# Delta-rule heads: the second weight tile's split ahead of the exponents' arguments, and the three engines' orders around it

## What is computed

```python
q, k, v = silu(conv(h @ w_q)), silu(conv(h @ w_k)), silu(conv(h @ w_v));  z = silu(h @ w_z)
q, k = l2norm(q) * 128**-0.5, l2norm(k)
gam = exp(G[t] - G[s]) below the diagonal          # G: running sum of the log decay in a chunk
A = strict(beta * (k @ k.T) * gam);  attn = (q @ k.T) * gam
X = inverse(I + A)                                 # u0 = X @ (v*beta), w = X @ (k*beta*exp(G))
for each chunk t:                                  # the state S is carried from chunk to chunk
    u = u0 - w @ S;  o = (q*exp(G)) @ S + attn @ u;  S = exp(G_last)*S + (k*exp(G_last-G)).T @ u
out = rmsnorm(o) * g_head * z
```

## Time and profile before

| | value |
|---|---|
| median of three runs | 1972.1 us |
| the profiled execution | 1974.02 us |
| its span, from first to last instruction | 1972.3 us |
| TensorE busy in the span | 1716.7 us (87%) |
| VectorE busy | 909.3 us (46%) |
| ScalarE busy | 614.8 us (31%) |
| GpSimd busy | 225.4 us (11%) |
| mean granted TensorE clock | 0.935 |

### The profile page before, as it was taken

One profiled execution on the slowest core, in us unless ns is written; L12 is line 12 of the kernel. 1 busy time (PEld: TensorE's weight loads), 2 busy tenths in 40 slices (PEclk: granted clock), 3 DMA queues, 4 the chain that ended last, 5 costly groups with the idle time before them and its releaser, 6 DMA issues. The chain is left out here.

```text
span 1972.3 us, 32281 instructions
## 1 busy us (share of the span) xinstructions
PE 1716.7 (87%) x11328; PEld 1496.0 (76%) x11328; DVE 909.3 (46%) x2004; ACT 614.8 (31%) x1523; POOL 225.4 (11%) x481
## 2 busy tenths in 40 slices
PE   6875999999699999899389997899899899877797
PEld 1124888888699999699278887888788788766696
DVE  0043344443355454512555554566566557563422
ACT  0033232322222322423533442333333333331422
POOL 0010000000000000000100000033133223222000
PEclk9986999999799999899688998999999999998798
DMA  6642241222223321141232211311111111010322
GB/s 243 233 142 64 60 113 49 74 54 69 62 61 82 96 53 53 33 133 43 73 90 73 70 32 49 89 34 49 36 36 45 36 36 45 4 37 1 95 86 69
DMA packets 194512, 138.16 MB, mean 70 GB/s; under 512 B 13310, under 2 KB 188346, under 8 KB 192262
## 3 DMA queue, kind: packets, MB, share of 16 engines
q1 hardware_dynamic: 179464, 127.76, 22.6%
q10 hardware_dynamic: 14976, 9.45, 1.6%
HBM read 126.06 MB, written 11.13 MB: 70 GB/s over the span
## 5 line engine op out<-in xcount | busy, mean ns | idle before, releaser
L160 PE MATMUL bank<-hT_low,gdn_w_high 128*128 128x288 f32 x512 | 173.4, 339 | 40.8 <-DVE gdn_w_low L1335 37.7
L161 PE MATMUL bank<-hT_high,gdn_w_low 128*128 128x288 f32 x512 | 156.7, 306 | 0.0
L162 PE MATMUL bank<-hT_high,gdn_w_high 128*128 128x288 f32 x512 | 156.5, 306 | 0.0
L160 PE MATMUL bank<-output_gT_low,output_w_high 128*128 128x288 f32 x512 | 154.2, 301 | 0.0
L161 PE MATMUL bank<-output_gT_high,output_w_low 128*128 128x288 f32 x512 | 152.5, 298 | 0.0
L162 PE MATMUL bank<-output_gT_high,output_w_high 128*128 128x288 f32 x512 | 152.4, 298 | 0.0
L160 PEld LDWEIGHTS bank<-hT_low,gdn_w_high 128*128 128x128 f32 x512 | 101.7, 199 | 51.4 <-issue 27.9
L1713 POOL TENSOR_TENSOR gdn_A_level<-gdn_AT,const 128x128 f32<-128x128 f32 (+1 forms) x232 | 110.0, 504 | 188.5 <-DVE gdn_AT L1635 112.8
L161 PEld LDWEIGHTS bank<-hT_high,gdn_w_low 128*128 128x128 f32 x512 | 102.1, 199 | 0.0
L162 PEld LDWEIGHTS bank<-hT_high,gdn_w_high 128*128 128x128 f32 x512 | 101.6, 198 | 0.0
L233 PE MATMUL bank<-setup_w_ada,setup_silu_c 128*2 128x512 f32 x192 | 90.1, 624 | 13.1 <-DMA setup_w_ada<-in_w_ada 13.1
(11 more groups left out here) (444 smaller groups left out, 4651.9 us busy)
## 6 DMA issues: line engine op xcount, KB each, us to landing
x<-in_w_in_even SPq DMA_DIRECT2D x72, 512.0 KB, 4.1
x<-in_w_in_odd SPq DMA_DIRECT2D x56, 512.0 KB, 4.0
setup_w_ada<-in_w_ada SPq DMA_DIRECT2D x16, 1536.0 KB, 6.7
output_w_out<-in_w_out_even SPq DMA_DIRECT2D x28, 256.0 KB, 3.5
output_w_out<-in_w_out_odd SPq DMA_DIRECT2D x28, 256.0 KB, 3.4
gdn_E<-G_rows SPq DMA_DIRECT2D x8, 576.0 KB, 4.9
x<-in_x_prompt SPq DMA_DIRECT2D x2, 2048.0 KB, 9.4
out_y_p<-x SPq DMA_DIRECT2D x1, 2048.0 KB, 6.8
```

What stands on the lines that cost most here:

```text
L160: pe.matmul(out, w[0], x[1], start=first, stop=False)
L161: pe.matmul(out, w[1], x[0], start=False, stop=False)
L162: return pe.matmul(out, w[0], x[0], start=False, stop=last)
```

## The change

TensorE's items are dealt out anew: one more ahead of the k and q transposes, two fewer between the k products and the first inverse's transposes, one more in the levels, and the last two behind the recurrence's last products. On VectorE `low` of tile 1 goes right behind z, the arguments of the exponents go behind `kq_norm`, and the scaled copies of k and v go behind `attn_ready`. On ScalarE the exponents go behind the copies of k^T and q^T. Nothing is added or left out.

```diff
-    LEVEL_FILL = (39, 40, 42, 43, 44, 45, 46, 47, 48, 49, 50, 51, 52)
+    LEVEL_FILL = (38, 39, 40, 41, 43, 44, 45, 46, 48, 49, 50, 51, 52)
...
-            project(pe, ahead, 5, 22)
+            project(pe, ahead, 5, 23)
...
-            project(pe, ahead, 22, 26)
+            project(pe, ahead, 23, 27)
...
-            project(pe, ahead, 26, 37)
+            project(pe, ahead, 27, 36)
             pe.wait_ge(*s["XT1_ready"].done(h, 0))
             pe.wait_ge(*s["attn_ready"].done(h, 0))
...
-            project(pe, ahead, 37, 39)
+            project(pe, ahead, 36, 38)
...
-                project(pe, ahead, *((52, 55), (55, 58), (58, 60), (60, 62), (62, 64))[t])
+                project(pe, ahead, *((52, 55), (55, 58), (58, 60), (60, 61), (61, 62))[t])
...
                 pe.matmul(PS[7][0:R, P:2 * P], tiles(atT, t), u[0:R, :], start=True, stop=True).then_inc(s["o_psum"].sem, 1)
+                if t == PT:
+                    project(pe, ahead, 62, 64)
                 if t:
                     turn_g(pe, h, t - 1)
```

```diff
             take_projection(act, ahead, 0)
-            act.wait_ge(*s["arg_ready"].done(h, 0))
-            act.activation(E[:, :, 0:SEQ], E[:, :, 0:SEQ], ACT.Exp).then_inc(s["E_ready"].sem, 1)
-            act.activation(E[0:DEC, :, SEQ:TOK], E[0:DEC, :, SEQ:TOK], ACT.Exp).then_inc(s["E_ready"].sem, 1)
             take_projection(act, ahead, 1)
...
             last.then_inc(s["kq_copied"].sem, 1)
+            act.wait_ge(*s["arg_ready"].done(h, 0))
+            act.activation(E[:, :, 0:SEQ], E[:, :, 0:SEQ], ACT.Exp).then_inc(s["E_ready"].sem, 1)
+            act.activation(E[0:DEC, :, SEQ:TOK], E[0:DEC, :, SEQ:TOK], ACT.Exp).then_inc(s["E_ready"].sem, 1)
             take_projection(act, ahead, 2)
```

```diff
             dve.scalar_tensor_tensor(zs[:], tz, 1.0, zr, ALU.add, ALU.mult).then_inc(s["z_ready"].sem, 1)
 
+            low(dve, ahead, 1)
+
+            dve.wait_ge(*s["rn_ready"].done(h, 0))
...
+            dve.tensor_tensor(qn[:], tk[:, :, 0, :], spread(sc[:, 1, :]), ALU.mult).then_inc(s["kq_norm"].sem, 1)
+
             dve.wait_ge(*s["G_loaded"].done(h, 15))
...
             last.then_inc(s["arg_ready"].sem, 1)
 
-            dve.wait_ge(*s["rn_ready"].done(h, 0))
...
-            dve.tensor_tensor(qn[:], tk[:, :, 0, :], spread(sc[:, 1, :]), ALU.mult).then_inc(s["kq_norm"].sem, 1)
-            low(dve, ahead, 1)
-            dve.tensor_tensor(sc[:, 2, :], sc[:, 0, :], gcol(1), ALU.mult)
...
-            dve.tensor_tensor(bv[:], tk[:, :, 2, :], spread(gcol(2)), ALU.mult).then_inc(s["kv_scaled"].sem, 1)
             low(dve, ahead, 2)
...
             dve.tensor_tensor(atT[:, 0:SEQ], PS[3][:, :], E[:, 0, 0:SEQ], ALU.mult).then_inc(s["attn_ready"].sem, 1)
+
+            dve.tensor_tensor(sc[:, 2, :], sc[:, 0, :], gcol(1), ALU.mult)
+            dve.tensor_tensor(sc[:, 3, :], sc[:, 0, :], gcol(3), ALU.mult).then_inc(s["scale_b"].sem, 1)
+            dve.wait_ge(*s["scale_b"].done(h, 0))
+            dve.tensor_tensor(kbe[:], tk[:, :, 1, :], spread(sc[:, 2, :]), ALU.mult)
+            dve.tensor_tensor(kg[:], tk[:, :, 1, :], spread(sc[:, 3, :]), ALU.mult)
+            dve.tensor_tensor(bv[:], tk[:, :, 2, :], spread(gcol(2)), ALU.mult).then_inc(s["kv_scaled"].sem, 1)
+
             dve.wait_ge(*s["X1_copied"].done(h, 0))
```

More of the change, by code:

```diff
@@ L1622, in dve_turn @@
             dve.tensor_tensor(qn[:], tk[:, :, 0, :], spread(sc[:, 1, :]), ALU.mult).then_inc(s["kq_norm"].sem, 1)
-            low(dve, ahead, 1)
-            dve.tensor_tensor(sc[:, 2, :], sc[:, 0, :], gcol(1), ALU.mult)
[L1625 to L1628, removed]
-            dve.tensor_tensor(bv[:], tk[:, :, 2, :], spread(gcol(2)), ALU.mult).then_inc(s["kv_scaled"].sem, 1)
+            dve.wait_ge(*s["G_loaded"].done(h, 15))
+            for i, name in ((1, "neg_strict"), (0, "neg_causal")):
+                for t in range(T):
+                    R = rows(t)
+                    at = E[0:R, i, t * P:t * P + R]
+                    last = dve.scalar_tensor_tensor(at, at, M["Gcol"][0:R, t, bass.ds(h, 1)],
+                                                    M.c(name, R)[:, 0:R], ALU.subtract, ALU.add)
+            last.then_inc(s["arg_ready"].sem, 1)
             low(dve, ahead, 2)
```

## The result

The changed kernel takes 1945.6 us (median of four, 1944.13 to 1948.81) against 1971.65 us of the kernel before (four runs): a ratio of 0.9868, 95% interval 0.9851 to 0.9885. A second measurement on another occasion gave 0.9864 (0.9843 to 0.9886). It is faster, as forecast, but by 26 us and not by 35: 1945.6 lies above the range of 1931 to 1943.

A forecast was written before the change was run, and what follows sets the result against it. Seven heads were held limited by TensorE's own queue, stopped mostly by waits for tile 1. 29.7 + 10.9 - 2.8 - 2.8 + 0.3 = 35.3 us gained gave a forecast of 1936.5 us, range 1931 to 1943.

The forecast's parts named there:

- the normalised q ended more than 0.3 us after item 22: Sign of being wrong: q comes over 0.3 us behind the last TensorE item placed ahead of the k and q transposes.
- TensorE waits in the levels for the inverse's updates: Sign of being wrong: TensorE waits for VectorE's updates in the levels, where nothing was expected to be late.
- The split of tile 1: VectorE's split moves 4.24 us earlier, so TensorE's wait for the tile goes: 29.7 us gained over seven heads.
- The clock: TensorE's clock no longer falls behind the wait for tile 1: 1.55 us a head, 10.9 us over seven heads.
- k and q normalised: Ahead of the k transposes: `kq_norm` comes 0.25 us earlier, GpSimd's power covering the split; at worst 0.2 us a head lost.
- The scaled copies of k and v: Their 2.49 us on VectorE fit its idle time between attn and the levels; nothing late, no cost.
- VectorE late in the levels: Rival: GpSimd's masked copies stretch the moved copies by 1.18, at worst 0.7 us a head, 1941.4 us; chance 0.15.
- Nine items ahead of the first inverse: Nine items instead of eleven leave TensorE a new 0.4 us wait for attn in seven heads: 2.8 us cost.
- Recurrence: At the fourth token tile, taking one item out lengthens TensorE's wait by 0.4 us in seven heads: 2.8 us cost.
- Levels: The levels get 14 items for 13; no cost beyond the items themselves if the inverse's updates come in time.
- Arguments and exponents: Moved later on VectorE and ScalarE; E is ready at 1350.3, before the k products end, hidden with 1.2 us to spare.
- the last head: It has no projection, so it gains only the 0.25 us by which `kq_norm` comes earlier.

The follow-up runs named there:

- norm_first: The changed kernel with VectorE's split of tile 1 put back behind the normalised q, still ahead of the exponents' arguments; 1979.7 us in one run.
- split_quarters: kv_after_split2 with the split of tile 1 made in four instructions instead of one, in the same place; 1942.5 us in the profiled execution.
- kv_after_split2: The changed kernel with the scaled copies of k and v and their two small scales moved behind the split of tile 2; 1937.8 us, ratio 0.9837.
- mask_waits: The changed kernel with GpSimd starting level 1's masked copies only when the scaled copies of k and v are done; 1940.3 us in one run.
- old_items: The changed kernel with TensorE's items dealt out as before the change, all else as changed; 1942.3 us in one run.
- exps_early: The changed kernel with ScalarE's wait for the arguments and its two exponents back ahead of the copy of group 1; 1973.7 us in one run.
- split_only: The kernel before with only VectorE's split of tile 1 moved right behind z; 1951.75 us, ratio 0.9875 to the kernel before.
- split_before_z: kv_after_split2 with the split of tile 1 ahead of z instead of behind it; 1946.2 us in the profiled execution.

## Why the prediction was wrong

The direction was right, and so was the mechanism of the gain; two steps that were costed at nothing or next to it were wrong, and 26 us came where 35.3 were summed. Two of the prediction's own signs of being wrong came true: the normalised q ended more than 0.3 us after item 22, and TensorE waits in the levels for the inverse's updates. Step by step:

- **The split of tile 1: right.** 30.4 us of waits fell to 0.9 (forecast 0.87 left in the first head). norm_first takes it away again and gets a wait of 4.09 us.
- **The clock: right.** It is 1.00 in each of the seven heads with a projection (0.98 in a middle head before). norm_first brings it back.
- **k and q normalised: this step failed.** It said that `kq_norm` comes 0.25 us earlier because the power, 1.97 us in the rows, covers the split. It took the power's duration from a place where ten operations of 0.25 us from start to start lay beside it and set one instruction of 1.2 us there. The power took 2.80, `kq_norm` came 0.65 us behind item 22, and the bound of "up to 0.2 us" was too small. Forecast 12.18 us from token to k transposes, measured 12.88: 0.7 us a head. norm_first (power back at 1.97 us) and split_quarters (2.00 us, and no wait for q) settle the cause.
- **The scaled copies of k and v: this step failed.** It said that the moved 2.49 us fit to the hundredth in VectorE's idle time. From the first scale (1349.17) they took until 1353.08, 3.9 us, and all of the 1.4 us more lay in two instructions of 128x5. Levels 0 and 1 took 10.5 us and not 9.47: 1.0 us a head, of which 0.8 go when the copies and GpSimd are kept apart (kv_after_split2, mask_waits) and 0.2 are the new deal's. The rival "VectorE late in the levels" had the cause, GpSimd's masked copies, and it happened. But its price was wrong: it scaled the copies by 1.18. What happened is that the small scale, which I had at 0.08 us from start to start, was held for 1.3, nearly as long as GpSimd's copies lasted, and the large copies ran behind them at their usual length. A factor on durations can't give that; the end of GpSimd's work could have. Before, the copies ended at 1358.01 + 4.46 = 1362.47, 1.5 us behind attn's end at 1360.93:

```profile
1358.01 4.46 POOL L1713 TENSOR_TENSOR gdn_A_level<-gdn_AT,const 128x128 f32<-128x128 f32 x10 [14.32 <-DVE gdn_AT L1635]
```

  mask_waits settles it. And the item taken out of level 0 made it dearer: with the old deal the same lateness costs 0.3 us (old_items).
- **Nine items ahead of the first inverse: right**, 6.72 against 6.67 us.
- **Recurrence: right in kind, too dear.** 0.25 us and not 0.4.
- **Levels: the extra item was dearer in the forecast than on the chip.** It was to cost its 0.41 us. Levels 2 to 5 took 17.12 us with nine items and with eight, but levels 0 and 1 in their new deal took 0.2 more (kv_after_split2): 0.2 us in all. A level with three items, 5.1 us, is followed by one of 4.49 instead of 4.68.
- **Arguments and exponents: right.** Nobody waited for E. The forecast didn't ask what the old place on ScalarE would cost now; exps_early says 3.5 us.

A middle head was to gain 5.0 us and gained 3.7: 0.7 us lost to the power's lateness and 0.8 to the scale's, 0.2 found in the levels and 0.15 in the recurrence. The seven heads took 503.2 us and take 476.5, a gain of 26.7 us, and the last head gained 0.7 where 0.25 were forecast: together the 27.4 us of the stage. I had put 0.15 on the rival that held a half of the truth and nothing on the other half: contention was looked for in one direction and at one pair of operations alone.

## What to carry to other kernels

A duration read in the trace holds only beside the neighbours that it was read with. When work of VectorE is moved, list what GpSimd does beside its new place. Price a GpSimd step by the length of the VectorE instruction beside it, and a short VectorE operation, at worst, by the time until GpSimd's run of instructions ends, not by a percentage. When one long VectorE instruction must lie beside a GpSimd step that somebody waits for, cut it into pieces: 0.2 us more on VectorE bought 0.8 us on GpSimd here. And before a redistribution is judged by its sum, run the one line that carries the gain by itself.

## What was not expected of the hardware

- GpSimd's power of 128x10 took 1.97 us with VectorE idle and beside VectorE operations of 0.25 us from start to start, 2.80 beside one of 1.22, 2.33 beside one of 0.75, and 2.00 beside the work of the 1.22 us in four instructions. VectorE's small scale of 128x5 took 0.15 us with GpSimd idle and 1.40 beside its masked copies, until almost their end. Yet the inverse's first factor has operations of 64x64 beside the same copies that took 0.43 us, and not 1.40. Why the small scale was held for several masked copies and those were not, no run here shows.
- The inputs may decide, but this is not shown. The Trainium skill ("GPSIMD Engine Reference", Specifications) names the contention with VectorE's instructions that have two SBUF inputs. The small scale, the split and z all have two, so the runs agree, and so does this contrast in the changed kernel:

```profile
1346.04 0.21 DVE L1633 TENSOR_TENSOR gdn_AT<-bank,gdn_E 64x64 f32<-64x64 f32 x1
...
1348.09 0.43 DVE L1640 TENSOR_TENSOR gdn_X_and_XT<-const,gdn_Q 64x64 f32<-64x64 f32 x1
1348.44 0.21 DVE L1641 TENSOR_TENSOR gdn_attnT<-bank,gdn_E 64x64 f32<-64x64 f32 x1
```

  L1633 and L1641 read one input from PSUM (`bank`). L1633 ran before GpSimd's copies began at 1346.32, L1641 beside them, and both took 0.21 us. L1640, beside the copies with both inputs in SBUF, took 0.43; how long it takes without them, no run shows.
- The clock fell in a few heads where no long wait preceded it. In mask_waits it went to the lower level once, in the recurrence, where TensorE's waits were at most 0.6 us, the same as in the changed kernel, whose clock stayed up. That stretch and the next lost 0.8 and 0.85 us:

```profile
1322.00:1324.00 2.00, 1.98 (x11) 1.16 (x11) 0.51 (x3) 0.71 (x4) 0.74 (x2) 1.00 0.11 33
1324.00:1326.00 2.00, 2.00 (x10) 1.71 (x10) 1.23 (x4) 0.29 (x2) 0.00 (x0) 0.71 0.00 0
1326.00:1328.00 2.00, 2.00 (x11) 1.98 (x10) 0.54 (x2) 1.28 (x4) 0.72 (x2) 0.50 0.15 45
```

  In split_only it fell behind a wait of 1.6 us in two heads and not in the five others, in split_before_z behind one of 1.35 us in the first head and not behind those of 1.15 us in five others, and two of split_quarters' recurrences show the same loss of 0.8 us as mask_waits. What decides is open; a sum made with the clock at full speed throughout is low by some us.
